# A hybrid decoder step on one core: in the page loop, the recurrence's matmuls and evacuations are put ahead of the next pages' turns

## Time and profile before

| what | value |
|---|---|
| median of three runs | 1763.18 us (1760.81 to 1764.95) |
| profiled execution, its own time | 1761.63 us |
| its span, first to last instruction | 1759.8 us |
| mean granted TensorE clock | 0.946 |
| PE busy | 1564.6 us, 89% |
| DVE busy | 912.0 us, 52% |
| ACT busy | 625.6 us, 36% |
| POOL busy | 24.0 us, 1% |

### The profile page before, as it was taken

How to read it: one execution, slowest core, us unless ns; L and a number is a source line. 1 busy time by engine, 2 the same in 40 slices (tenths; PEclk the granted TensorE clock), 3 DMA queues, 4 the chain that set the end, 5 groups by cost and what they waited for, 6 DMA issues and landing times. The chain is left out here.

```text
span 1759.8 us, 32857 instructions
## 1 busy us (share of the span) xinstructions
PE 1564.6 (89%) x11615; PEld 1272.0 (72%) x11615; DVE 912.0 (52%) x1876; ACT 625.6 (36%) x1612; POOL 24.0 (1%) x53
## 2 busy tenths in 40 slices
PE   2999677639998999999999988999888999998999
PEld 1599434428888888788878874534444999998998
DVE  2311477766867676777767671333566222224221
ACT  3022233454545454545544550000224233334121
POOL 0000000020000000000000000000000000000000
PEclk8999886869999999999999998899899999999999
DMA  7022000022313121222223107134203233331331
GB/s 240 1 72 72 16 0 1 18 72 61 98 36 91 45 80 54 71 61 62 73 52 84 39 1 274 43 93 183 82 1 97 77 90 95 95 95 41 89 103 55
DMA packets 190630, 128.24 MB, mean 73 GB/s; under 512 B 49240, under 2 KB 176081, under 8 KB 190468
## 3 DMA queue, kind: packets, MB, share of 16 engines
q1 hardware_dynamic: 190476, 126.36, 25.0%
HBM read 120.03 MB, written 6.37 MB: 72 GB/s over the span
## 5 line engine op out<-in xcount | busy, mean ns | idle before, releaser
L1350 PE MATMUL bank<-wka,turned 128*128 128x260 f32 x1536 | 250.3, 299 | 24.4 <-ACT arena L1518 13.0
L1350 PEld LDWEIGHTS bank<-wka,turned 128*128 128x128 f32 x1536 | 199.7, 189 | 51.9 <-issue 30.4
L1350 PE MATMUL bank<-wkb,turned 128*128 128x256 f32 x1536 | 224.6, 282 | 0.0
L1350 PEld LDWEIGHTS bank<-wkb,turned 128*128 128x128 f32 x1536 | 201.6, 189 | 0.0
L1667 DVE CAST turned<-bank 128x256 fp32r<-128x256 f32 x258 | 109.3, 424 | 163.9 <-PE bank L1350 116.4
L1684 DVE TENSOR_REDUCE arena<-arena 128x4 f32<-128x512 f32 x256 | 173.0, 676 | 1.2 <-ACT arena L1520 0.9
L1517 ACT ACTIVATE arena<-bank 128x256 f32<-128x256 f32 x256 | 97.7, 382 | 196.8 <-PE bank L1350 195.5
L2287 PE MATMUL bank<-h_high,ffn_high 128*128 128x260 f32 x704 | 142.5, 284 | 3.0 <-DVE h_low L2345 3.0
L2287 PE MATMUL bank<-h_low,ffn_high 128*128 128x260 f32 x704 | 142.8, 284 | 0.0
L2287 PE MATMUL bank<-h_high,ffn_low 128*128 128x260 f32 x704 | 142.1, 284 | 0.0
L1761 PE MATMUL bank<-arena,yT 128*128 128x512 f32 (+1 forms) x240 | 121.0, 641 | 4.6 <-DMA arena<-in_w_mix_out 4.1
(11 more groups left out here) (411 smaller groups left out, 2566.1 us busy)
## 6 DMA issues: line engine op xcount, KB each, us to landing
arena<-in_cache_mla_ckv SPq DMA_DIRECT2D x256, 128.0 KB, 2.0
arena<-in_ffn_w_gate SPq DMA_DIRECT2D x22, 512.0 KB, 4.1
arena<-in_ffn_w_up SPq DMA_DIRECT2D x22, 512.0 KB, 5.2
arena<-in_ffn_w_down SPq DMA_DIRECT2D x16, 704.0 KB, 4.6
arena<-in_w_in SPq DMA_DIRECT2D x16, 512.0 KB, 3.9
arena<-in_cache_mla_kpe SPq DMA_DIRECT2D x256, 32.0 KB, 1.8
arena<-in_x_prompt SPq DMA_DIRECT2D x8, 512.0 KB, 6.5
arena<-in_w_mix_out SPq DMA_DIRECT2D x2, 2048.0 KB, 10.4
```

The lines of the kernel that those rows point to most:

```text
L1350: last = nc.tensor.matmul(dst, t[:, (2 * part + k) * P:(2 * part + k + 1) * P], w4[:, wpart, k, cl], start=(m == 0), stop=(m == len(SPLIT) ...
```

## The change

On PE, `gdn(p)` moves from behind the turns and the value matmuls to directly behind product n. On DVE, `gdn(n)` in even slots moves ahead of `take_next(n+2)` and `sum_squares(n)`; in odd slots it stays where it was. ACT, POOL and SP keep their order. No instruction is added or taken away, and no wait of a semaphore is changed.

```diff
@@ tensor
                     for p in range(PAGES // 2):
                         n = 2 * p
                         page_products(i, r, n)
+                        gdn(p, b)
                         rope_scores(i, r, n)
                         turn_next(i, r, n + 2)
                         for part in (n - SLOT_PV, n - SLOT_PV + 1):
@@
                         if n == SLOT_QD + 1:
                             latent(b, 1 - r)
-                        gdn(p, b)
                         page_products(i, r, n + 1)
@@ vector
                     for n in range(PAGES):
+                        if n % 2 == 0:
+                            gdn(n, b)
                         take_next(i, r, n + 2)
                         sum_squares(i, r, n)
-                        gdn(n, b)
+                        if n % 2 == 1:
+                            gdn(n, b)
                         soften(n, b, 1 - r)
```

## The result

The changed kernel is slower. Its median is 1783.8 us (1781.0 to 1789.8, four runs) beside 1763.8 us of the kernel before; the ratio is 1.0124, with a 95% interval of 1.0100 to 1.0149. The forecast was 1777 in a range of 1757 to 1788. The profiled execution took 1784.55 us, with a span of 1782.7.

A forecast was written before the change was run, and what follows sets the result against it. PE was taken to bound the page loop, so only waits and seams could change. The terms 0.40 + 0.43 + 0.55 + 0.45 gave 1.83 per batch, 14.6 us over eight, hence 1777 us in a range of 1757 to 1788.

The forecast's parts named there:

- What bounds the loop: Page loop: PE is the bound; only waits and seams can change; a better order gives at most 30.5 us, 1.7%.
- Quiet pairs: Pairs 4 to 10: no cost, a pair stays 4.55 us, with 0.5 of cover for page n+2's evacuation.
- Term A: Pairs 0 to 3: product 2 newly waits about 0.97 for ACT, product 6 waits 1.4; +0.40 us per batch.
- My sign of being wrong: In batch 1's timeline, a step from product to `gdn` of 1.4 or 1.7 us instead of 1.5.
- Term B: Pairs 11 and 12: products 24 to 26 come later behind DVE's and ACT's longer pieces; +0.43 us per batch.
- Term C: Pairs 13 to 15: product 28 newly waits 0.44 for DVE's late evacuation, L1446 is 0.3 late; +0.55 us per batch.
- Term D: Pairs 3 to 7: one more seam each at 0.09; +0.45 us per batch, from 0 to 0.85.
- Rival 1: Pairs 0 to 3, 11 to 15: waits are filled and not moved; about 1763 us, chance 0.13.
- Rival 2: Turns' evacuation waits go under `gdn`, exponentials begin 0.39 earlier; 1.25 less per batch, about 1752 us, chance 0.13.
- Rival 3: Every seam behind a product is dear, 0.17 in 15 pairs on top of the sum; about 1797 us, chance 0.08.

The follow-up runs named there:

- values_beside: The changed kernel with the value matmuls of pairs 3 to 7 directly behind gdn(p), ahead of rope and turns: 1780.0 us, ratio 1.0115.
- table_first: The changed kernel with ACT's Ln piece of slot 0 and its table load ahead of take_rope: 1778.5 us, ratio 1.0097.
- long_old_beside: The changed kernel with the old order in pairs 0 and 11 to 15, and pairs 3 to 7's values directly behind gdn(p): 1761.5 us, ratio 1.0003.
- pair2_only: The kernel before with PE's new order in pair 2 alone, gdn(2) directly behind product 4: 1756.7 us, ratio 0.9978.

## Why the prediction was right, and where its sizes were off

The forecast of the direction and of the places was right, and 1783.8 lies in the range. The size was too small: 14.6 us forecast, 24.1 in the traced loop, 20.1 between the medians. Every term came out larger than forecast, none smaller, so no errors cancelled.

**What bounds the loop.** Right: PE's work stayed, and only waits and seams changed. But of the 30.5 us of waits that I called the most a better order could give, 5.2 stand at the loop's turns and 0.5 ahead of its first product, where no order of a pair reaches them.

**Quiet pairs.** Right, shown by the kernel with the new order in quiet pairs alone. The table has +0.05 for pairs 8 to 10.

**Term A**, pairs 0 to 3, forecast +0.40. Measured over pairs 0 to 2 it is +0.81 in the third batch and +0.68 in the second (batch 1). The mechanism (ACT's load behind the turns, L1518 freeing bank 2) was right, shown by moving the load. The size was off since I booked the two seams as even within the pair. They are, but 0.19 of them stands ahead of the turns: ACT's table load starts 4.39 after product 0 (477.96 - 473.57) where I had 475.50 - 471.32 = 4.18, and pair 0 grows by 1.16 and not 0.97. In batch 1 pair 2 gives back 0.47 where I had 0.57, and that is the rest. My sign of being wrong, a step from product to `gdn` of 1.4 or 1.7 and not 1.5, half came true: it is 1.60.

**Term B**, pairs 11 and 12, forecast +0.43, measured 0.58 - 0.11 = +0.47. **Term C**, pairs 13 to 15, forecast +0.55, measured 0.53 - 0.16 + 0.33 = +0.70. Each wait stands where it was named. In pair 13 the +0.53 for my 0.44 is the 0.09 by which `gdn` starts later behind its product, 1.60 and not 1.51, with DVE's chain behind it. The remaining 0.03 to 0.04 each of pairs 14, 15 and of term B I did not take apart.

**Term D**, the seam, forecast +0.45, measured +0.96, 0.19 in each of five pairs. This is the term that was mis-sized most: I took 0.09 from the step of a turn to the next matmul. But a seam has a price on the far side too, where the weight load no longer runs ahead of the matmul, 0.10 more. The upper end that I gave, 0.85, was still too low. The Trainium skill ("TensorEngine Tiling (Array Packing)", section "Tiling Modes") says that a change of the tiling mode drains TensorE. The trace agrees in that two such changes in a quiet pair cost the same in either order, and that the pairs with one more take 0.19 longer; a drain itself is in no row.

**Not foreseen**: 0.65 us more at the loop's three turns together.

The sum: 0.81 + 0.47 + 0.70 + 0.96 + 0.05 = 2.99 a batch, 23.9 for eight, against 1.83 and 14.6. With 0.65 for the turns it is 24.6, against the measured 24.1 of the loop; the first batch and those with r = 1 lose a little less than the one in the table. Rival 1, waits filled and not moved, holds for none of the three places. Rival 2 (the gain of 1.25 a batch) exists in pair 2 alone, where it is 0.24 to 0.47; in the changed kernel ACT and DVE are late at all the points that it named. Rival 3 is out: it had 0.17 more in every pair, and a pair without values grew by 0.02.

## What to carry to other kernels

Moving a step of a dense queue ahead of another doesn't save its time, it delays the other by it. So list who waits for the one that is passed, and add all that stands behind it in that engine's queue; a table load behind a wait for a turned page cost a product 1.07 us a batch here, and moving it gave back 0.8 to 0.9 of pairs 0 to 2. Take a new order only in those places where the old one had a wait: pair 2 alone won where all sixteen pairs lost 20 us. If two engines' orders belong together, change both or none. Count how often PE's queue leaves the 128x128 tile, before and after.

## What was not expected of the hardware

- Leaving the 128x128 tile for a group of smaller matmuls and coming back cost 0.19 us: 0.09 from a product to a 64-row matmul, and 0.10 in which the next weight load does not run ahead of its matmul. Smaller tiles of two kinds behind each other (values and recurrence) cost it once.
- The releaser that the profile names can be the wrong one of two that ended close together: L1669 ended at 480.13, L1518 0.15 before, and the experiment showed it was the latter.
- PE stood idle for 1.5 to 2.6 us at a turn of the loop, and the length differs from turn to turn in one trace (2.11, 2.06 and 1.67 in the changed kernel's). Nothing here was tried on it, and its cause stays open.
- Behind some of these turns PE went on at the lower clock. In the kernel before the granted clock is 0.50 from 720.20 to 722.90, the fifth batch, and one turn follows the next in 0.21 us and not 0.11; pair 0 takes 6.95 for 5.39. The same is seen once in the changed kernel, twice in values_beside, table_first and long_old_beside, and once in pair2_only, each worth 1.3 to 1.6 us. PE had been idle for 1.8 to 2.6 us before each of them, but also for 2.11 before a batch without it. No run here shows what decides, and as it comes in some batches and not in others, it moves single executions by a few us against what the pairs sum to.
